# Splitting each 1 MB weight load into two halves, each requested when its own block's low part is made, in a one-core decoder layer with dense product-key experts

## The reference, cut to what matters

```python
def block(xb):
    q = (xb @ w_q).reshape(TOKEN_BLOCK, PEER_HEADS, 2, PEER_HALF)
    s = jnp.einsum('thcd,hcnd->thcn', q, sub_keys).astype(jnp.float32)
    vals, idx = lax.top_k(s, PEER_TOPK)
    cand = vals[:, :, 0, :, None] + vals[:, :, 1, None, :]
    ...
    g = jax.nn.softmax(best, axis=-1)
    u = u_tab[ids]
    v = v_tab[ids]
    h = jax.nn.gelu(jnp.einsum('td,thkd->thk', xb, u))
    w = (g * h.astype(jnp.float32)).astype(xb.dtype)
    return jnp.einsum('thk,thkd->td', w, v)
```

## Time and profile before

| | |
|---|---|
| median of 3 runs | 3744.37 us (3740.94 to 3750.39) |
| profiled execution, its own time | 3754.39 us |
| its span in the trace | 3752.6 us |
| mean granted TensorE clock | 0.994 |
| TensorE matmul busy | 3651.6 us (97%), 19704 matmuls |
| VectorE busy | 2615.3 us (70%) |
| ScalarE busy | 1273.1 us (34%) |
| GpSimd busy | 1690.2 us (45%) |
| DMA | 873.48 MB, mean 233 GB/s |
| value stage, first to last addition into `res` | about 2485 to 3507 us |

### The profile page before, as it was taken

The page is one execution under the profiler, slowest core; times in us unless marked ns, Lnnn a source line. Parts: engine busy times, 40 slices in busy tenths (PEclk is TensorE's granted clock), DMA queues, the critical chain, the costliest instruction groups (busy, mean ns, idle before and its releaser), DMA issues.

```text
span 3752.6 us, 55122 instructions
## 1 busy us (share of the span) xinstructions
PE 3651.6 (97%) x19704; PEld 3311.9 (88%) x19704; DVE 2615.3 (70%) x4018; ACT 1273.1 (34%) x1659; POOL 1690.2 (45%) x1044
## 2 busy tenths in 40 slices
PE   8999999999999899999999999999999999999999
PEld 6888888877888689999999999999899999999777
DVE  3555555553411699977898888778899888898722
ACT  4334333443112523344433333232233232232532
POOL 4444444434444245668777776623322222223143
PEclk9999999999999999999999999999999999999999
DMA  5333334333433123488999999888889988898232
GB/s 182 125 124 127 129 129 129 129 109 121 151 140 123 68 89 113 157 318 306 352 376 380 371 361 340 325 325 353 345 349 350 338 337 331 345 347 332 97 109 81
DMA packets 189061, 873.48 MB, mean 233 GB/s; under 512 B 29296, under 2 KB 70448, under 8 KB 97456
## 3 DMA queue, kind: packets, MB, share of 16 engines
q1 hardware_dynamic: 98128, 496.61, 36.6%
q0 software_dynamic: 59360, 340.13, 23.6%
q10 hardware_dynamic: 31488, 35.66, 2.6%
HBM read 813.38 MB, written 58.90 MB: 232 GB/s over the span
## 4 chain that ended last, share of the span: by engine, by line
PE 49%; DVE 17%; DMA 13%; DVEq 7%; POOL 7%; issue 5%; ACT 2%; ACTq 0%; SPq 0%; POOLq 0%
PE bank L648 16%; PE bank L650 15%; PE bank L649 15%; DMA raw<-ws 10%; DVEq L1651 5%; POOL expert_spill L584 4%; DVE wlo L1575 3%; DVE yacc L1677 2%; POOL urows L602 2%; DVE yx L1689 1%; DVE hot L1521 1%; ACT whi L1022 1%; DMA expert_spill<-gval,goff 1%; DVE sc L1384 1%; DMA urows<-u_tab,idx 1%
## 5 line engine op out<-in xcount | busy, mean ns | idle before, releaser
L1022 ACT ACTIVATE whi<-raw 128x1024 fp32r<-128x1024 f32 x784 | 820.9, 1057 | 2273.7 <-DMA raw<-ws 1156.7
L648 PE MATMUL bank<-ahi,whi 128*128 128x352 f32 (+1 forms) x3968 | 1428.0, 360 | 42.9 <-DVE wlo L1575 17.5
L650 PE MATMUL bank<-ahi,wlo 128*128 128x352 f32 (+1 forms) x3968 | 1416.5, 357 | 0.0
L649 PE MATMUL bank<-alo,whi 128*128 128x352 f32 (+1 forms) x3968 | 1413.8, 356 | 0.0
L561 POOL TENSOR_TENSOR wlo<-raw,whi 128x1024 fp32r<-128x1024 f32 x316 | 788.7, 2500 | 1066.3 <-ACT whi L1022 1053.8
L648 PEld LDWEIGHTS bank<-ahi,whi 128*128 128x128 f32 x3968 | 751.5, 189 | 139.4 <-issue 32.2
L650 PEld LDWEIGHTS bank<-ahi,wlo 128*128 128x128 f32 x3968 | 749.6, 189 | 77.4
L649 PEld LDWEIGHTS bank<-alo,whi 128*128 128x128 f32 x3968 | 749.1, 189 | 72.7 <-issue 0.5
L648 PE MATMUL bank<-xwhi,whi 128*128 128x352 f32 x2048 | 668.0, 326 | 35.0 <-DVE wlo L1575 30.4
L650 PE MATMUL bank<-xwhi,wlo 128*128 128x352 f32 x2048 | 661.9, 323 | 0.0
L649 PE MATMUL bank<-xwlo,whi 128*128 128x352 f32 x2048 | 659.8, 322 | 0.0
(11 more groups left out here) (229 smaller groups left out, 2700.2 us busy)
## 6 DMA issues: line engine op xcount, KB each, us to landing
raw<-ws SPq DMA_DIRECT2D x394, 1024.0 KB
hg<-expert_spill SPq DMA_DIRECT2D x58, 704.0 KB, 9.6
expert_spill<-zero SPq DMA_DIRECT2D x32, 704.0 KB, 7.8
expert_spill<-hst ACTq DMA_DIRECT2D x128, 176.0 KB
gate_spill<-gout ACTq DMA_DIRECT2D x32, 256.0 KB, 2.1
gl<-gate_spill SPq DMA_DIRECT2D x32, 256.0 KB, 2.7
expert_spill<-gval,goff POOLq DMA_INDIRECT x384
hg<-expert_spill POOLq DMA_DIRECT2D x6, 704.0 KB, 5.9
```

The source lines that it names most:

```text
L648: pe.matmul(ps_out, hi, xh, start=first, stop=False)
L649: pe.matmul(ps_out, hi, xl, start=False, stop=False)
L650: return pe.matmul(ps_out, lo, xh, start=False, stop=last)
L1022: act.activation(whi[:, s], raw[:, s // 2, s % 2], ACT.Copy).then_inc(hi_done, 1)
```

## The change

A unit now comes in two transfers of 512 KB, one for each block (4 KB contiguous for each partition). Each has its own semaphore (four in place of two), and each is asked for when the low part of the block that held the same half slot is made, where before both low parts were waited for. ScalarE's high part waits for its own half's semaphore.

```diff
-        raw_in = [sem("raw_in0"), sem("raw_in1")]
+        raw_in = [sem(f"raw_in{i}") for i in range(4)]
...
-                sp.wait_ge(lo_done, 2 * u + 2)
-                sp.dma_start(raw[:, s], ws[nxt]).then_inc(raw_in[s], 16)
+                for half in range(2):
+                    sp.wait_ge(lo_done, 2 * u + (half + 1))
+                    sp.dma_start(raw[:, s, half], ws[nxt, :, half]).then_inc(raw_in[2 * s + half], 16)
...
-            sp.dma_start(raw[:, 0], ws[0]).then_inc(raw_in[0], 16)
+            for half in range(2):
+                sp.dma_start(raw[:, 0, half], ws[0, :, half]).then_inc(raw_in[half], 16)
...
-            sp.dma_start(raw[:, 1], ws[1]).then_inc(raw_in[1], 16)
+            for half in range(2):
+                sp.dma_start(raw[:, 1, half], ws[1, :, half]).then_inc(raw_in[2 + half], 16)
...
-                act.wait_ge(raw_in[s // 2], unit)
+                act.wait_ge(raw_in[s], unit)
...
-                act.wait_ge(raw_in[s // 2], 16)
+                act.wait_ge(raw_in[s], 16)
```

## The result

The changed kernel took 3706.15 us (median of 4 runs, 3696.72 to 3707.02), the kernel before 3744.26 (4 runs); the ratio is 0.9879, 95% interval 0.9860 to 0.9899. Run again later beside other kernels it took 3712.8 us (6 runs) against 3749.59, ratio 0.9903 (0.9882 to 0.9924). The forecast was 3706 us in a range of 3688 to 3738.

A forecast was written before the change was run, and what follows sets the result against it. The `raw` slot's round was taken to bound the value stage; 34 us there plus 2, 1 and 1 elsewhere made 38, so 3706 us from the median of 3744.4, range 3688 to 3738.

The forecast's parts named there:

- The bound: Value stage: the `raw` slot's round takes 16.72 and 18.13 us, where TensorE's pace allows 15.4.
- The even half may take long to land: Value stage: a half lands in 6 to 8 us; up to 12.8 us makes nobody wait.
- allowance of 12.8 us: Value stage: time a half may take to land, from a 15.4 us turn with 2.6 us of other work.
- VectorE is late next: Value stage: VectorE sets groups 2, 3 and 14 at 62.8 us; TensorE groups 1 and 4 to 13 at 61.7.
- Bandwidth: Value stage: groups 4 to 13 need 355 GB/s, groups 2 and 3 382, against at most 383 in the expert stage.
- The 6 us given back: Value stage: deducted from a 40 us gain for 12-row groups at the bandwidth edge and granted clock below 1, leaving 34.
- The small terms: Outside the value stage's 15 groups: 2 us in the first expert stage, 1 at the start, 1 in group 15.
- the 1 us of the forecast: Start of the kernel: the first half lands before the whole does, ScalarE's first high part begins earlier, gaining 1 us.
- Bandwidth in the place of the round: Rival: halves and fetched rows bunch, landings stretch, value stage gains 17 us instead of 34; 3728 us, chance 0.17.
- Nothing: Rival: VectorE's wait is only taken over by another, such as `hg` or ScalarE's order; 3744 us, chance 0.08.
- Short turns in a shared queue: Rival: shorter packets alternate with fetched rows, costing 45 us in the first expert stage; 3796 us, chance 0.09.
- the shorter runs: Weight loads: each partition's run falls from 8 KB to 4 KB, costed at nothing since `xin` loads reach 434 GB/s.

The follow-up runs named there:

- first profile: Profile of the changed kernel from its first measurement, against the kernel before: 3706.15 us, ratio 0.9879.
- second profile: Profile of the same changed kernel, unaltered, when run again later beside other kernels: 3712.8 us, ratio 0.9903 to the kernel before.
- whole units: Kernel before, still with 1 MB transfers, but VectorE makes both low parts ahead of the fetched rows in the value stage: 3708.99 us, ratio 0.9884.
- quarters: Changed kernel with each half in two transfers of 256 KB (2 KB contiguous for each partition), asked for at the same moment: 3711.85 us, ratio 0.9905.
- late halves: Changed kernel with both 512 KB halves asked for only when both low parts are made: 3723.27 us, ratio 0.9930 to the kernel before.

## Why the prediction was right

**The bound.** That the value stage turned with the round of the `raw` slot held at every test: taking the rows out of the round by a split or by VectorE's order gives the same time, and leaving them in keeps about a third of the gain from coming. The reading that led there was the chain of waits, not the shares of busy time: TensorE was at 97% and the DMA share at 0.90, and neither names a round.

**The even half may take long to land.** I took 6 to 8 us for a half and said that it hardly matters below 12.8. Asked for early, an even half had landed a median of 7.1 us after its issue over the value stage of the first profile, inside the 6 to 8. In groups 1 to 3, where the DMA share is highest, it took longer than a late one and not less: the mean is 8.6 us, the longest 11.7, and in the second profile 9.1 and 12.8. So once the allowance of 12.8 us was all but used up. The mean round there is 15.6 us and 15.5, the pace of TensorE.

**VectorE is late next.** Its pace was right and its price was not. 62.8 us were forecast for a group of 12 rows, and group 2 took 63.04; in the three other profiles with early requests in this stage and the rows in their old place it took 63.03 or 63.04, whatever TensorE's rate. Group 1, forecast as TensorE's at 61.7, was VectorE's too: its 11 rows make 3 x 9.07 + 5 x 6.63 = 60.36, and it took 60.37. But a group is cut at VectorE's own additions, and TensorE had no wait in groups 1 to 4. VectorE fell behind in the 12-row groups and its backlog was gone in the next ones: groups 1 to 4 took 249.0 us together, where TensorE's pace and the 3.5 us of `sum_extra` make 250.3 and the forecast had 252. So the 12-row groups cost the stage nothing. Group 14 took 61.60. Group 0 took 66.82 (66), and groups 4 to 13 612.7 us (618), or 620.3 at the slower rate.

**Bandwidth.** The edge was where it was put: groups 2 and 3 moved 380 and 386 GB/s at shares of 0.97 and 0.99, against 382 forecast. It gave no gap. The 6 us given back for it and for the clock were too many: without them the forecast for the 15 groups was 936 us, and the second profile of the change, at the rate of the kernel before, has 933.9.

**The sum.** Its terms were off in both directions. The value stage gave 49.3 us instead of 34 in the profiled pair, of which TensorE's rate is some part: the second profile of the change has the 15 groups in 3422.82 - 2488.90 = 933.9 us, 42.4 less than 976.3. So the term was too small by about 8 us against this profile of the kernel before, which was itself 10 us above its median; where those 10 us lay, no run shows. The small terms, 4 us in all, were not there: the stage begins at 2485.26 us where it began at 2485.16, and between 2482.95 and 2488.90 in the nine profiles. In the first expert stage TensorE's wait for low parts went from 17.5 us to 22.7, which in the seven other profiles is 13.7 to 24.8, with whole units (20.5) as with quarters (13.7). It does not follow the change. At the start the first half did land earlier, and ScalarE's first high part began at 6.45 us where it had begun at 7.49, the 1 us of the forecast. It bought nothing, because the activations `xin` bound the start. The chain of waits after, and TensorE's first matmul of a block after and before:

```profile
3.39 5.95 DMA xin<-xT
9.36 1.07 ACT ahi L1069
10.53 2.81 DVE alo L1336
```

```profile
13.47 0.77 PE L651 MATMUL bank<-ahi,whi 128*128 128x512 f32 x1 [8.93 <-DVE alo L1336]
```

```profile
12.21 0.76 PE L648 MATMUL bank<-ahi,whi 128*128 128x512 f32 x1 [7.74 <-DVE alo L1333]
```

The activations' first high part began at 9.36 us (9.40 before) and VectorE's first low part of them at 10.53 (10.54 before). That low part then took 2.80 us where it had taken 1.52, and TensorE began its first block 1.3 us later, not 1 us earlier. GpSimd's low part of the second weight block now runs from 9.90 us beside it, where it began at 10.94; whether that is why VectorE's was slower was not tried. I had costed an earlier load without asking what waits beside it.

That the sum came out is in part chance. The medians fell by 38.1 us and, in the second comparison, by 36.8, beside a forecast of 38. The profiled span fell by 49 us, because the profiled execution of the kernel before took 3754.4 us, more than any of its three first runs, and that of the change did not stand above its own median; from 3754.4 the sum gave 3716, and 3705.35 was measured. A stage term that was too small and small terms that were not there made up for each other.

**The rivals.** Bandwidth in the place of the round: not seen. Nothing: excluded by the interval. Short turns in a shared queue: the quarters, with twice as many packets again, would have cost over 300 us and cost nothing that can be told. I had costed the shorter runs at nothing; in the first expert stage they took 4% more of the engines' time for a byte at 4 KB and 12% at 2 KB, and 1% in the value stage, in a resource that does not bind. The Trainium skill's rule to batch transfers to at least 1 MiB (DMA: Bandwidth & Descriptors, under Bandwidth) would have kept the whole units; the trace agrees in so far as there is such a price, and disagrees on what it is worth here. The fit of 2.0 us plus bytes over 436 GB/s, which the prediction gives beside that rule, stands in another section of the same page of the Trainium skill (Anatomy of one DMA) and is measured there for DMAs issued by GpSimd; these are issued by SP. At the start, with no fetched rows moving, the first half let ScalarE begin 1.04 us sooner (6.45 against 7.49), near the 1.2 of the fit.

**What stays open.** How the gain divides between the moment and the length has only the coarse answer of the late halves and of the groups, one profile each, since shortening a landing and advancing a request work on the same round and neither can win more than TensorE's pace allows. Why TensorE's rate has steps was not tried.

## What to carry to other kernels

Where the chain of waits comes back to the same transfer at the same distance, write down everything between its landing and the next request, and compare the sum with the pace of the bounding engine. What stands there without need (here two fetched rows and the other block's low part) can be taken out by splitting the buffer's release, or, as cheaply, by changing the order of the engine that releases it; doing both added nothing that could be told here. Half a transfer doesn't land in half the time in a busy queue (8.1 us against 8.7 here), but half a microsecond less in a round that is one or two over the pace is already much of the gain; the earlier request counts where the round is longest. And where a group's length is cut at the additions of one engine, it shows that engine's pace and not what the group costs: look whether the bounding engine waits.

## What the runs showed of the hardware that was not expected

In stretches of unbroken 352-column matmuls at a granted clock of 1.00, TensorE started 622 or 623, 627, or 631 or 632 in 100 us, and one execution could have two of them in turn (627 in the first expert stage and 623 in the value stage). One program showed 631 and 623 in the same stage in two executions. In the value stage it goes with the execution and not with the kernel, and between these two it made 6.9 us over 15 groups; over all 6144 matmuls of the stage it would be 12 us (986 against 974, an estimate from the two rates). Whether the same holds in the first expert stage is open: there it was 627 in six profiles of split loads, and 622 or 623 in one of split loads and in both of whole units.
